# Hybrid decoder block on one core: the bias rows of the first expert layer loaded once, one lane each, and VectorE's expert loop written out

## What is computed

```python
def clamped_swiglu(h):
    h_glu, h_lin = h[..., ::2], h[..., 1::2]
    h_glu = jnp.minimum(h_glu, SWIGLU_LIMIT)
    h_lin = jnp.clip(h_lin, -SWIGLU_LIMIT, SWIGLU_LIMIT)
    return h_glu * jax.nn.sigmoid(SWIGLU_ALPHA * h_glu) * (h_lin + 1.0)
...
    def run_block(args):
        tok, e = args
        h = x_pad[tok] @ w1[e] + b1[e]
        return clamped_swiglu(h) @ w2[e] + b2[e]
```

## Time and profile before

| | |
|---|---|
| median of 3 runs | 1349.53 us (1349.27 to 1350.82) |
| profiled execution, its own time | 1348.86 us |
| its span in the profile | 1347.1 us |
| mean granted clock of TensorE | 0.987 of full speed |
| PE busy | 1236.4 us, 92% of the span |
| DVE busy | 338.3 us, 25% |
| ACT busy | 199.1 us, 15% |
| read from HBM | 447.99 MB |
| share of the span in the chain that ended last | PE 43%, SP's queue 32%, DMA 17%, DVE 4% |

### The profile page before, as it was taken

How to read it: one execution, slowest core, us unless ns; L and a number is a source line. 1 busy time by engine, 2 the same in 40 slices (tenths; PEclk the granted TensorE clock), 3 DMA queues, 4 the chain that set the end, 5 groups by cost and what they waited for, 6 DMA issues and landing times.

```text
span 1347.1 us, 16403 instructions
## 1 busy us (share of the span) xinstructions
PE 1236.4 (92%) x6534; PEld 592.8 (44%) x6534; DVE 338.3 (25%) x574; ACT 199.1 (15%) x381; POOL 0.2 (0%) x4
## 2 busy tenths in 40 slices
PE   7999989999989999999998989898998989898985
PEld 6886778888453333333332323232332323232321
DVE  1156463211122123122221212122221212121122
ACT  1225422100111011110111101010110111010112
POOL 0000000000000000000000000000000000000000
PEclk9999989999989999999999999999999999999998
DMA  9343102694549999999999999999999999999992
GB/s 346 110 155 122 64 3 65 225 396 144 206 176 402 417 417 416 417 416 416 417 417 418 418 418 418 417 417 416 418 417 417 418 418 418 416 415 415 413 416 103
DMA packets 95357, 449.72 MB, mean 334 GB/s; under 512 B 8624, under 2 KB 21040, under 8 KB 62544
## 3 DMA queue, kind: packets, MB, share of 16 engines
q1 hardware_dynamic: 95008, 447.99, 83.2%
q10 hardware_dynamic: 304, 1.08, 0.3%
HBM read 447.99 MB, written 1.05 MB: 333 GB/s over the span
## 4 chain that ended last, share of the span: by engine, by line
PE 43%; SPq 32%; DMA 17%; DVE 4%; issue 3%; ACT 1%; ACTq 0%; PEldq 0%; DVEq 0%
PE ps L460 41%; SPq L425 17%; DMA upper<-in_w_exp 9%; SPq L417 7%; DMA ring<-in_w_exp 7%; SPq L414 7%; DVE ring L1381 0%; DVE upper L1472 0%; PE ps L695 0%; SPq L410 0%; DMA xrows<-in_x 0%; PE ps L933 0%; ACT ring L1133 0%; PE ps L476 0%; ACTq L1237 0%
## 5 line engine op out<-in xcount | busy, mean ns | idle before, releaser
L460 PE MATMUL ps<-ring,upper 128*64 128x512 f32 (+4 forms) x2928 | 585.1, 538 | 46.4 <-DMA ring<-in_w_exp 40.5
L460 PEld LDWEIGHTS ps<-ring,upper 128*64 128x64 f32 (+2 forms) x2928 | 176.7, 138 | 405.3 <-issue 289.1
L460 PE MATMUL ps<-upper 128*64 128x512 f32 (+6 forms) x1592 | 278.8, 443 | 24.6 <-DMA upper<-in_w_exp 16.1
L460 PEld LDWEIGHTS ps<-upper 128*64 128x64 f32 (+4 forms) x1592 | 135.1, 162 | 169.7 <-issue 109.3
L460 PE MATMUL ps<-xT,ring 128*128 128x256 f32 x640 | 142.8, 381 | 0.0
L460 PEld LDWEIGHTS ps<-xT,ring 128*128 128x128 f32 x640 | 120.5, 190 | 17.6 <-issue 1.3
L1646 DVE TENSOR_TENSOR upper<-ps,upper 128x512 f32<-128x512 f32 x32 | 22.1, 692 | 364.1 <-PEq L913 364.1
L1666 DVE TENSOR_TENSOR xrows<-xrows,ps 128x1024 f32<-128x1024 f32 x32 | 39.1, 1222 | 264.5 <-PE ps L460 264.5
L1256 ACT ACTIVATE upper<-upper 128x512 f32<-128x512 f32 x32 | 20.2, 631 | 566.1 <-DVE upper L1649 566.1
L1262 ACT ACTIVATE factors<-ps 64x512 f32<-64x512 f32 x64 | 37.9, 593 | 211.8 <-PEq L928 211.1
L460 PE MATMUL ps<-factors,upper 128*128 128x512 f32 x128 | 63.2, 617 | 1.5 <-ACT factors L1262 1.5
(11 more groups left out here) (210 smaller groups left out, 499.9 us busy)
## 6 DMA issues: line engine op xcount, KB each, us to landing
ring<-in_w_exp SPq DMA_DIRECT2D x288, 1024.0 KB, 21.4
upper<-in_w_exp SPq DMA_DIRECT2D x96, 1024.0 KB, 22.5
ring<-in_w_gate SPq DMA_DIRECT2D x8, 1024.0 KB, 5.0
ring<-in_w_in SPq DMA_DIRECT2D x8, 896.0 KB, 11.2
ring<-in_w_branch SPq DMA_DIRECT2D x6, 1024.0 KB, 5.3
ring<-in_w_in SPq DMA_DIRECT2D x8, 640.0 KB, 3.9
ring<-in_w_mem_kv SPq DMA_DIRECT2D x4, 1024.0 KB, 4.9
upper<-in_w_gate SPq DMA_DIRECT2D x4, 1024.0 KB, 11.0
```

The source lines that it names most:

```text
L460: return pe.matmul(o, l, r, start=start, stop=stop, skip_group_check=True)
```

## The change

1. **Loads.** `load_w1` no longer issues bias transfers, and no longer waits for `b1_spread` or signals `b1_due`. ACT issues four transfers in the place of its four at L1237: each now brings 32 half rows (128 KB), one expert to a partition, so that expert e's row stands in partition e of each group of 32 (first halves in the groups at 0 and 32, second halves at 64 and 96). All 32 rows lie in the first half of the tile `merged`, and one semaphore counts the four.
2. **Shuffle.** `spread_bias` copies partition e of each group, with the mask `[e] * 32`. It waits for the load once, at the first expert. Its output, `b1all`, moves from the tile `upper` to the second half of `merged`.
3. **DVE's loop.** The mask is fixed when the program is built, so that the loop over the pairs 1 to 14 is a Python loop: 13 pairs which were a loop of the machine are written out.
4. The wait for `stored` at a later pass falls away; no later pass is executed with these inputs.

```diff
-        b1rows = merged[:].rearrange("p (e b) n -> p e (b n)", e=2)
-        b1all = kb(110, 4)
+        b1rows = merged[:, 0:2, :].rearrange("p b n -> p (b n)")
+        b1all = merged[:, 2:4, :].rearrange("p b n -> p (b n)")
...
-            def load_w1(q, a, r, zero=False, bias=True):
+            def load_w1(q, a, r, zero=False):
 
                 g = q * (NE // GROUP) + a
                 for c in range(KC):
                     s, _, n = w1_place(c, g, r, zero)
-                    if c == 0 and bias:
-                        sp.wait_ge(b1_spread, g * GROUP + (r - 1))
-                        sp.sem_inc(b1_due, 1)
                     sp.wait_ge(slots_used, n + (NMIX - RING + 1))
-                    if c == 0 and bias:
-                        for twice in range(2):
-                            at = 32 * twice
-                            sp.dma_start(b1rows[at:at + 65:64, r % 2, :],
-                                         b_exp1[0, bass.ds(a * GROUP + r, 1), :].rearrange("a (h f) -> (a h) f", h=2))\
-                              .then_inc(b1_full[r % 2], 16)
...
-                    for e in range(2):
-                        for twice in range(2):
-                            at = 32 * twice
-                            act.dma_start(b1rows[at:at + 65:64, e, :], b_exp1[0, e:e + 1, :].rearrange("a (h f) -> (a h) f", h=2))\
-                               .then_inc(b1_full[e], 16)
+                    for quarter in range(4):
+                        hf = quarter // 2
+                        act.dma_start(b1rows[NE * quarter:NE * quarter + NE, :], b_exp1[0, :, hf * D:(hf + 1) * D]).then_inc(b1_full, 16)
...
-            def spread_bias(E, N, parity, very_first=False):
-
-                dve.wait_ge(b1_full[parity], (N + 1) * 32)
-                if not very_first:
+            def spread_bias(E, e, very_first=False):
+
+                if very_first:
+                    dve.wait_ge(b1_full, 64)
+                else:
                     dve.wait_ge(up_read, E)
                 dve.sem_inc(b1_here, 1)
-                dve.stream_shuffle(b1all, b1rows[:, parity, :], [0] * 32).then_inc(b1_spread, 1)
+                dve.stream_shuffle(b1all, b1rows, [e] * NE).then_inc(b1_spread, 1)
...
             def one_pass(q, very_first=False):
-                if not very_first:
-                    dve.wait_ge(stored, q * (TT * 16))
                 select(q, 0, q * NPAIR, very_first)
                 pair(q, 0, True, False, very_first)
-                if very_first:
-                    pair(q, 1, False, False, False, True)
-                    with dve.Fori(2, NPAIR - 1) as k:
-                        pair(q, k, False, False)
-                else:
-                    with dve.Fori(1, NPAIR - 1) as k:
-                        pair(q, k, False, False)
+                for k in range(1, NPAIR - 1):
+                    pair(q, k, False, False, False, very_first and k == 1)
```

More of the change, by code:

```diff
@@ L290, in build @@
         lora_loaded, sink_loaded, late_loaded = sem("lora_loaded"), sem("sink_loaded"), sem("late_loaded")
-        b1_full = [sem("b1_full0"), sem("b1_full1")]
+        b1_full = sem("b1_full")
         root, root_m, scaled, scaled_m = sem("root"), sem("root_m"), sem("scaled"), sem("scaled_m")
@@ L324, in build @@
             sem("prod_sb"), sem("act_sb"))
-        b1_due, b1_here, b1_spread, glu_raw, lin_sb = (sem("b1_due"), sem("b1_here"), sem("b1_spread"), sem("glu_raw"),
-                                                       sem("lin_sb"))
+        b1_here, b1_spread, glu_raw, lin_sb = sem("b1_here"), sem("b1_spread"), sem("glu_raw"), sem("lin_sb")
         actT_ps, actT_sb, down_ps, yrow_sb, selg_raw, selg_sb, selgT_ps, selgT_sb, sc_ps, acc_sb = (
@@ L427, in load_w2, with load_group @@
                       .then_inc(slot_full[s], 16)
-            def load_group(q, a, count=GROUP, bias_from=0):
+            def load_group(q, a, count=GROUP):
                 for r in range(count):
-                    load_w1(q, a, r + 1, False, r >= bias_from)
+                    load_w1(q, a, r + 1)
                     load_w2(q, a, r)
             def load_pass(q, very_first=False):
-                load_w1(q, 0, 0, True, not very_first)
+                load_w1(q, 0, 0, True)
                 if very_first:
-                    load_group(q, 0, GROUP, 1)
+                    load_group(q, 0)
                 with sp.Fori(1 if very_first else 0, NE // GROUP - 1) as a:
@@ L1687, in pair @@
                     select_gates(q, k - 1, N - 1, second)
-                spread_bias(E, N, 0, very_first)
+                spread_bias(E, 2 * k, very_first)
                 swiglu(E, very_first)
-                spread_bias(E + 1, N, 1)
+                spread_bias(E + 1, 2 * k + 1)
                 if very_first:
```

## The result

The comparison gives 1340.65 us for the changed kernel (median of 4 runs, 1339.56 to 1340.88) against 1350.09 us (4 runs, 1349.27 to 1350.82), a ratio of 0.9929 with a 95% interval of 0.9912 to 0.9946: faster by 9.4 us in the medians. The predicted time was 1340.8 us. The profiled execution took 1340.88 us with a span of 1339.1 us, 8.0 us less than the profiled one of before.

What follows compares the result with a forecast made beforehand. From about 500 us DMA bytes set the pace, with three engines late from bias transfers. Terms -9.1 (late engines), +0.2 (ACT's issues), +0.2 (written-out loop) sum to -8.7 from 1349.53: 1340.8 us, range 1337.0 to 1346.0.

Steps and rivals of the forecast that it cites:

- (a): Tail of the DMA transfers: 1.69 MB landing after 1315 us, shared evenly, would end near 1319.1, not 1328.3: -9.2 us.
- (b): First w1 chunk behind a bias pair lands a 0.43 us step late; over 26 pairs -11.2 us.
- (c): Bias bytes alone: two 4 KB rows on one DMA engine take 0.31 us, 26 times: -8.2 us.
- SP's waits and queue time at nothing: SP's queue: removing bias issues (about 5 us an expert) and the `b1_spread` wait gains nothing beyond the late engines' term.
- ACT's issues, +0.2: ACT's four larger bias loads, on the critical chain before PE's copies: +0.2 us, bounds 0 to +3.0; their 0.52 MB hidden.
- DVE's waits at nothing: DVE's shuffle waited 92.6 us for the bias, but the next addition waited for PE's scatter: gain 0.
- The written-out loop, +0.2: DVE's program grows from 357 to 857 rows, fetched by the same DMA engines: +0.2 us, bounds 0 to +3.
- the rival of late code: DVE's code fetch queues behind weights, stalling DVE, `swiglu` and PE: +13.5, 1363 us; chance 0.05.
- another reason: Late engines have a cause other than bias transfers, such as the row-size turn; only bytes go: 1348.5 us; chance 0.12.
- doesn't do what it says: Bias transfers merely moved elsewhere under the weights; the prediction held it excluded by instruction order and gave no chance.
- Only part of the step: Last engine keeps its own delay or is hit by fetches; about half the lag stays: -4.5, 1345.0 us; chance 0.13.
- The whole step goes: The whole step behind bias pairs disappears and nothing replaces it, plus 1.0 us of bytes: -12.2, 1337.3 us; chance 0.12.

Runs made afterwards that it cites:

- e2: The changed kernel with two bias-shaped transfers (2 rows of 4 KB) per expert put back into SP's queue, into memory nothing reads: 1349.35 us, ratio 0.9995 to the kernel before.
- e5: The changed kernel with only SP's old wait for `b1_spread` and its signal put back, no extra transfers: 1340.61 us, ratio 0.9931 to the kernel before.
- e1: The kernel before with DVE's loop over the pairs written out and nothing else changed: 1348.70 us, ratio 0.9992.
- e4: The changed kernel with two transfers per expert put back, each one 4 KB row to partition 0 (32): 1345.18 us, ratio 0.9963 to the kernel before.
- e9: The changed kernel with two transfers of two 4 KB rows per expert put back, landing on partitions 0 and 4 (32, 36): 1345.91 us, ratio 0.9970 to the kernel before.

## Why the prediction was right, point by point

1. **Single DMA engines late by the bias transfers: right,** shown by e2 against e5 and e1. Of its three prices, (a) -9.2 came nearest to the comparison (-9.4, interval -7.3 to -11.9); the profiled pair shows -7.5 at the last landing. Its reason was not fully right. It took the tail's bytes as shared evenly, the last landing at 1319.1 to 1319.3; in the profile after it is at 1320.83, because 16 engines with equal bytes still end up to 3.8 us apart. In the forecast's own terms: from 1313 us on the rows hold 2 x (418 + 385 + 213 + 55) = 2.14 MB, which shared evenly would end at 1318.1 us. That is 1.0 us before the even end of before, just the 1.0 us of bytes that the forecast left out. But the last landing comes 2.7 us behind this even end, where the forecast allowed 0.2. That the landing is as late as 1320.83 is in part this one execution, whose weights came some 2 us later up to 535 us; in e5, which differs by a wait that costs nothing, the row reads

```profile
1300.49 18.90 DMA ring<-in_w_exp
```

   and the landing is at 1319.39 us, though there too it trails the even end by 2.9 us (2 x (412 + 238 + 72) = 1.44 MB from 1313 us on). (b), the step of 0.43 us behind a bias pair, was read well: the pace fell by 0.475 us. The 120.7 us forecast for four experts are (b)'s too; the -9.1 of the sum would have been 121.0, and 120.48 were measured. As a sum of the whole gain, 26 x 0.475 = 12.4, it is too large by the some 3 us that an engine trails anyway. (c), bytes alone, has the right size for a row in its own engine's place (e4, e9: 0.31) and is too small for this kernel's, which land elsewhere. So (a) hit as the difference of two things that the forecast did not have apart, a larger gain in pace and a spread that gives part of it back. That the forecast met the median within 0.2 us is luck: four executions of the changed kernel alone lie 1.3 us apart, and of the profiled pair the spans differ by 8.0 us where the medians differ by 9.4.

2. **SP's waits and queue time at nothing: right.** e5 measures the wait (0.9931 against 0.9929). w2 issues still take about 4.2 us each (16.74 for four).

3. **ACT's issues, +0.2: too high by 0.2.** 1.96 us against 2.68 for the four, and `up` at 386.06 us against 386.08. The nearest row, one issue of this form behind other transfers on SP (1.41 us), was the wrong measure for a queue that is nearly empty. The 0.52 MB were hidden, as said: 8 GB/s in the 10 us from 380 us.

4. **DVE's waits at nothing: right.** The wait moved on to the additions.

5. **The written-out loop, +0.2: nothing that can be measured** (e1, 0.9983 to 1.0002). The code came in four more packets of the second fetch queue (0.09 to 0.12 MB), not in 16 KB fetches as the prediction had costed them, and the rival of late code did not occur: the shuffles of the written-out code have no idle time before them (0.0 us), and so none that nothing ends.

The rivals: "another reason" and "doesn't do what it says" are excluded by e2 and e5. "Only part of the step" had its half lag in no run of the changed kernel, though what it described, a delay that stays on the last engine, is there with 3.8 us. "The whole step goes" had the right pace and left out the engines' natural spread. Of the signs to look for, one was missed: the fall in the tail took from about 1316 to 1321 us, not 2 to 3 us.

## What to carry to other kernels

Where large transfers keep all DMA engines full, the time is that of the fullest engine, so that a small transfer among them costs its bytes on the one or two engines that carry it, more where it lands on another engine's partitions, times the number of repeats: 16 KB per expert, 0.13% of the bytes, cost 0.7% here. Look at the tail of the transfers in stretches of 2 us: steps at one, two or three engines' rate say that, and the time by which the last landing trails an even share of the tail's bytes is an estimate of the gain before anything is changed (9.2 us here, 9.4 measured). Load such rows once, ahead, in many partitions; if they must go among the rest, keep each row on the partitions that its engine writes anyway (tried here for partitions 0 and 4 only), and count from the gain what the engines' own spread at the end gives back.

## What was not expected of the hardware

- Two transfers of one 4 KB row per expert cost 0.31 us on the partitions of the engine that carries them (0 and 32), 0.18 us from row to row. On another's (64 and 96, or 4 and 36) they are 0.31 us apart and make two engines late, by 0.44 and 0.28 us, the second without carrying anything; 8 KB packets over 345 ns go from 10 to 127 and 134.
- Spreading each transfer of 8 KB over 16 adjacent partitions, meant to balance the engines, slowed all of them by 0.15 us per expert, twice what its packets take.
- 32-byte rows on the same queue, with the same waits, cost nothing (0.9933 against 0.9929).
- With twice the transfers the other engines ran dry once the lag had grown to about 10 us, and the total rate fell from some 415 to as low as 403 GB/s, while the lag grew no further.
